# Order of the streamed high and low matmuls: runs of four instead of pairs

## The reference

```python
h = rmsnorm(x, g_mix); z = h @ w_in            # conv, q, k, v, forget and gate columns
merged = gc * (conv_y @ w_conv_out) + ga * (attn @ w_attn_out)
x = x + merged @ w_mix_out
h = rmsnorm(x, g_mlp)
x = x + square(relu(h @ w_ff1)) @ w_ff2        # 8192 wide
x = rmsnorm(x, g_final)
# second layer: modulation from c @ w_ada, MoBA attention beside an SSD mixer
# (in2 columns), out2, then a gated convolutional FFN (5632 wide: up, down), final norm
```

## Time and profile before

| | |
|---|---|
| median of three runs | 2555.27 us |
| profiled execution | 2556.62 us, its span 2554.8 us |
| TensorE matmuls (PE) | 2521.1 us busy, 99%, 14366 matmuls |
| TensorE weight loads (PEld) | 2181.6 us, 85% |
| VectorE (DVE) | 2016.2 us, 79% |
| ScalarE (ACT) | 1304.3 us, 51% |
| mean granted TensorE clock | 0.996 of full speed |
| HBM read | 562.26 MB, 221 GB/s over the span |

### The profile page before, as it was taken

The page is one execution under the profiler, slowest core; times in us unless marked ns, Lnnn a source line. Parts: engine busy times, 40 slices in busy tenths (PEclk is TensorE's granted clock), DMA queues, the critical chain, the costliest instruction groups (busy, mean ns, idle before and its releaser), DMA issues. The chain is left out here.

```text
span 2554.8 us, 47103 instructions
## 1 busy us (share of the span) xinstructions
PE 2521.1 (99%) x14366; PEld 2181.6 (85%) x14366; DVE 2016.2 (79%) x3099; ACT 1304.3 (51%) x2043; POOL 73.9 (3%) x78
## 2 busy tenths in 40 slices
PE   8999999999999999999999999999999999999997
PEld 7888888888888888888888888888888888888886
DVE  7778775689887887887889776676888888888888
ACT  5444444565553453544555554554546546446456
POOL 0000000000000000000000016300000000000000
PEclk9999999999999999999999999999999999999999
DMA  7785874557888888888886555545456656556554
GB/s 277 266 279 197 281 261 159 183 188 259 275 287 282 278 286 276 282 283 279 280 281 218 184 176 177 160 154 178 154 188 176 205 173 190 194 170 207 188 164 156
DMA packets 161749, 565.19 MB, mean 221 GB/s; under 512 B 18403, under 2 KB 18716, under 8 KB 161692
## 3 DMA queue, kind: packets, MB, share of 16 engines
q1 hardware_dynamic: 132428, 459.04, 54.0%
q10 hardware_dynamic: 27792, 101.20, 12.1%
q0 software_dynamic: 1472, 4.23, 0.6%
HBM read 562.26 MB, written 2.13 MB: 221 GB/s over the span
## 5 line engine op out<-in xcount | busy, mean ns | idle before, releaser
L304 PE MATMUL bank<-H,w_hi 128*128 128x512 f32 (+1 forms) x4480 | 1415.2, 395 | 12.2 <-DVE w_lo L1278 9.9
L1227 DVE TENSOR_TENSOR w_lo<-w_raw,w_hi 128x1024 fp32r<-128x1024 f32 x900 | 1092.3, 1222 | 143.8 <-ACT w_hi L734 138.4
L304 PEld LDWEIGHTS bank<-H,w_lo 128*128 128x128 f32 x4416 | 830.8, 188 | 190.8
L734 ACT ACTIVATE w_hi<-w_raw 128x1024 fp32r<-128x1024 f32 x900 | 912.5, 1051 | 12.4 <-PE bank L304 5.7
L304 PE MATMUL bank<-H,w_lo 128*128 128x256 f32 x4416 | 871.7, 278 | 0.0
L304 PEld LDWEIGHTS bank<-H,w_hi 128*128 128x128 f32 x4480 | 691.5, 189 | 20.7 <-issue 15.1
L304 PE MATMUL bank<-U,w_hi 128*128 128x512 f32 x1984 | 627.8, 396 | 2.4 <-DVE w_lo L1227 1.3
L755 ACT ACTIVATE scratch<-bank 128x256 f32<-128x256 f32 x356 | 136.9, 385 | 735.2 <-PE bank L304 735.2
L304 PEld LDWEIGHTS bank<-U,w_lo 128*128 128x128 f32 x1984 | 372.6, 188 | 86.5
L304 PE MATMUL bank<-U,w_lo 128*128 128x256 f32 x1984 | 401.7, 281 | 0.0
L304 PEld LDWEIGHTS bank<-U,w_hi 128*128 128x128 f32 x1984 | 308.0, 188 | 7.0 <-DVE w_lo L1227 3.5
(11 more groups left out here) (223 smaller groups left out, 1124.0 us busy)
## 6 DMA issues: line engine op xcount, KB each, us to landing
w_raw<-in_w_ff SPq DMA_DIRECT2D x256, 512.0 KB, 5.1
ada_w<-in_w_ada ACTq DMA_DIRECT2D x192, 512.0 KB, 4.6
w_raw<-in_w_up SPq DMA_DIRECT2D x176, 512.0 KB, 3.8
w_raw<-in_w_z SPq DMA_DIRECT2D x96, 512.0 KB, 4.8
w_raw<-in_w_in SPq DMA_DIRECT2D x88, 512.0 KB, 4.1
w_raw<-in_w_gate SPq DMA_DIRECT2D x64, 512.0 KB, 4.6
w_raw<-in_w_down SPq DMA_DIRECT2D x64, 384.0 KB, 3.1
w_raw<-in_w_down SPq DMA_DIRECT2D x64, 320.0 KB, 3.3
```

What stands on the lines that cost most here:

```text
L304: return nc.tensor.matmul(out, lhsT, rhs, start=start, stop=stop, skip_group_check=True)
L734: A(w_hi[:, slot, :], w_raw[:, slot, :], ACT.Copy).then_inc(sem("w_high"), 1)
L1227: TT(w_lo[:, slot, :], w_raw[:, slot, :], w_hi[:, slot, :].bitcast(F32), ALU.subtract)\
```

## The change

In `unit`, the chunks of a piece are taken in runs of four. In the first run (c0 = 0) the four high matmuls come first and then the four low ones, in the second (c0 = 4) the four low ones and then the four high ones. Before, the order alternated by chunk: high, low for an even chunk and low, high for an odd one. The wait for the operand is made once for a run, for all its chunks, where it was made for two chunks at a time. The increment of `piece_used` is still on the last matmul of the piece.

```diff
-                    for c in range(n):
-                        if par == 0 and operand and c % 2 == 0:
-
-                            pe.wait_ge(sem(operand), operand_base + k0 + min(c + 2, n))
-                        if c % 2 == 0:
-                            high(c)
-                            end = low(c)
-                        else:
-                            low(c)
-                            end = high(c)
+                    for c0 in range(0, n, 4):
+                        run = range(c0, min(c0 + 4, n))
+                        if par == 0 and operand:
+
+                            pe.wait_ge(sem(operand), operand_base + k0 + run[-1] + 1)
+                        for part in (high, low) if c0 % 8 == 0 else (low, high):
+                            for c in run:
+                                end = part(c)
                     end.then_inc(sem("piece_used"), 1)
```

## The result

The changed kernel takes 2559.79 us (median of 15 runs, 2557.87 to 2560.99) against 2555.27 us before (15 runs, 2553.19 to 2556.44): ratio 1.0019, 95% interval 1.0011 to 1.0026. It is slower by about 4.5 us, small but clear of zero, and 0.4 us from the forecast. The stated range, 2535 to 2580 us, is ten times as wide as the change and holds the times of all rivals but one (2581), so lying in it tests little. The inside of the forecast holds less well than its total, as the traces show.

A forecast was written before the change was run, and what follows sets the result against it. TensorE's matmul stream was taken as the bound. From the median 2555.3 us, + 7.0 on H, - 3.8 on U and B and + 0.9 for waits made + 4.1, so 2559.4 us, range 2535 to 2580 us.

The forecast's parts named there:

- Bound: TensorE, busy 2521.1 of 2554.8 us: the matmul stream itself is the bound, no producer late on average.
- Rates in a run: Runs of eight: high 231 ns, low 118.7, so 349.7 a chunk against 348.1 on H: + 7.0 us.
- U and B: Stages where U or B moves: 349.7 instead of 351.3 ns over 2344 chunks, - 3.8 us.
- My check sentence: Chunks take 349.7 ns in both kinds of stage; today's 3 ns difference between H and U should vanish.
- Waits: Operand waits for four chunks at once: mix + 0.7 us, first ff unit + 0.2; + 0.9 us taken.
- the longer stall: Mix stall grows to some 1.4 us; a half clock after it would cost 3.4 us, left out.
- Low runs are load-bound: Rival: in runs low takes 120 ns, high stays 233, 353 a chunk; + 26 us, 2581 us; chance 0.27.
- The alternation costs: Rival: width switches disturb the stream; steady runs settle at high 226, low 120; - 20.6 us, 2535 us; chance 0.23.
- An interval depends on its matmul only: Rival: order does not matter, 348.1 and 351.3 ns stay, waits leave + 0.9 us, 2556 us; chance 0.17.

The follow-up runs named there:

- e5: Kernel before, old order, with the area holding U, G, B and Z moved 32 bytes on in each partition: 2547.80 us, ratio 0.9971.
- e8: Changed kernel (runs of four) with the 32 bytes of padding behind Z taken out: 2554.98 us, ratio 0.9999 against the kernel before.
- e12: Kernel before, old order, with the 32 bytes of padding moved from behind Z to between H and the weights: 2566.24 us, ratio 1.0043.
- e10: Against e8, the low matmul of unit uses only 64 of its 128 weight columns, still moving 256: 2524.55 us, one run.
- e7: Kernel before, old order, with the 32 bytes of padding behind Z taken out: 2547.28 us, ratio 0.9970.
- e11: Against e8, the low matmul of unit moves 192 of its 256 columns, with the weight load whole: 2500.45 us, one run.
- e4: Kernel before, with high then low for every chunk, so the width changes at every matmul: 2568.21 us, ratio 1.0053.

## Why the prediction was right, and where it was not

**Bound.** Right: the stream of matmuls is the bound, and stream plus waits account for the total within 1 us.

**Rates in a run.** On H, taken 231 and 118.7; measured 230.4 and 119.0. Both came from the neighbours' rows. For high that is the mechanism too: unsettled intervals and then settled ones, five and three where I took six and two. For low the mean is right and the shape is not: I took six at 118.3 and two at 120, and the run has 113.5, 119.0 and then 120 from the third on. That the mean comes out is in part luck. The term was + 7.0 us and is 0.83 x 4352 = 3.6: its two rates are off by - 0.6 and + 0.3 ns and the base was 348.1, read over 32 chunks, where all pieces have 348.5. Small errors, multiplied by 4352.

**U and B.** The step that failed: "349.7 - 351.3", the same run rate for all stages. All the run rows stood on H or wn; none had U moving, and the 3 ns between H and U were taken to vanish without a reason for them. The term was - 3.8 us and is + 0.8. e5 to e8 and e12 show why: on U and B the moving operand lay 32 bytes off the weights, where runs do not settle. My check sentence, that the difference between H and U should vanish, is what failed in the trace (349.3 and 351.7). The two errors, - 3.4 and + 4.6, nearly cancel, and that the total is so close is luck.

**Waits.** Mix + 0.7 and the first ff unit + 0.2, both as in the rows; branch, ff2 and the opening show none. The clock did not fall after the longer stall.

**Rivals.** "Low runs are load-bound" was half right in mechanism: low goes to 120 on H, and half a load makes it 113.3 (e10), but high does gain. That fits the reason that I gave for dearer low runs, a load without a high matmul to cover it. "The alternation costs" had a true core, the settled 227 and 120, but only the last three of eight high matmuls reach 227, and on U none does, so the change made the kernel slower and not faster. "An interval depends on its matmul only" is out: the first low matmul of a run on H takes 113.5 ns and the last 119.9. The Trainium skill, page "TensorE: Matmul & The Clock Gate", section "Back-to-back issue gap", gives an isolated gap that depends on the columns N alone, N / 2.4 + 2.5 ns. By that no order would matter; measured, the same 4352 chunks take 348.2 to 350.0 ns in four orders, and what stands over N / 2.4 is 13.3 ns in settled runs of these fp32r matmuls with a load of 128 columns each.

## What to carry to other kernels

A stream of matmuls with a fresh load each had settled and unsettled rates here, and a run rate measured on one operand did not hold for another that lay elsewhere in memory. Before reordering, compare stages that do the same work with different tiles: 351.3 against 348.5 ns stood in the rows from the start and was worth more (7 us, one line) than the order. Compare starts, never busy time, when the pattern of overlap changes.

## What the runs showed of the hardware

- A moving operand shifted by 32 bytes against its weights, out of step within 64 bytes, costs 2.8 ns a chunk of 512 + 256 columns in the order of before (e5, e7 and e12 against before), nearly all of it in the 256-column matmul (118.5 against 115.4 ns), and runs do not settle (e8 against after). The period of 64 bytes is not shown.
- In settled runs a matmul of N columns takes N / 2.4 + 13.3 ns with a load of 128 columns (512 and 256 moved) and + 6.7 ns with 64 (e10, one run); at 192 moved it takes 109 to 116 ns, well over that sum (e11, one run). At the half clock a chunk takes its 640 ns of streaming and nothing more (before, 1711 us).
- With a change of width at every matmul (e4) the uneven pattern costs 353 ns a chunk and the even one 346.7 (231 and 115.7), 1.8 below the order of before. Why blocks of pieces enter one or the other, and whether e4 without the padding would keep the even one everywhere, was not tried and stays open.
